# Latent attention's projections as split products: query, key and value weights in the common weight ring, cached keys split before the last path block

## The chip, the cores and the metric

The kernel runs on one core of one Trainium2 chip. The metric is the device time of one launch in microseconds (us). TensorE (PE in the profile, its weight loads PEld) does the matrix products, VectorE (DVE) and ScalarE (ACT) the elementwise work and most copies out of PSUM, GpSimd (POOL) a share of the elementwise work between SBUF tiles, and SyncE (SP) issues most transfers. SBUF is the working memory on the chip, PSUM the accumulators that TensorE writes.

## The reference

Two layers of a hybrid block are applied to 512 latent and 128 context tokens, in 32-bit floats. Three branches are fed by one input projection: a long convolution, a differential attention and multi-head latent attention (MLA). Each is multiplied by a gate, projected, and merged. The change is in MLA:

```
c_q  = rms_norm(mla_dq, q_norm)                    # (tokens, 384)
qm   = (c_q @ w_uq).reshape(n, 8, 64 + 32)         # q_nope | q_rope
c_kv = rms_norm(mla_dkv, kv_norm)                  # (tokens, 256)
ckv_all = concat([cached_ckv, c_kv])               # latent tokens: 128 cached rows + 512
kv   = (ckv_all @ w_ukv).reshape(n, 8, 64 + 64)    # k_nope | v
s    = (q_nope . k_nope + rope(q_rope) . rope(k_rope)) * scale
y    = softmax(s) @ v
```

## The kernel before

Everything is stored with features on the 128 partitions and the 640 tokens along the free side. A matrix product of 32-bit floats is done in one of two ways.

Split products. `project` (L806) takes a weight block of 128 output features by 1024 (or 512) inputs. The weights come into a ring `W` of three buffers (`weight`, L665, by SP). ScalarE writes the high part `Wh` in the type float32r (`high_part`, L1213), and GpSimd (for a few blocks VectorE) the low part `Wl` = W - Wh (`low_part`, L1963). The activations are split in the same way beforehand (`Hh`, `Hl` for the layer's input, `BRh`, `BRl` for a gated branch). For each input block and each half of 320 tokens there are three products: Wh.xh (L817), Wh.xl (L818), and, after a wait for the low part, Wl.xh (L822). `Wh` and `Wl` have two buffers, so the high part of block n+1 waits for block n-1 to be done (`tile_done`). The ring buffer is loaded again when its low part is written.

Direct products. Attention, transposes and, before the change, MLA's own projections pass 32-bit tiles to TensorE as they are. `mqr` (rotary part, 2 blocks of 128 features) and `mqn` (other part, 4 blocks) multiply `wuq` by `cq` (L1140), `mk` (4 blocks) and `mv` (3 steps of two token blocks) multiply `wukv` by `ckv` (L1148, L1129). Their weights are loaded whole, once in a layer, at step (dqkv, 3).

Order. `layer_steps` writes the order of a layer out by hand as a list of steps, and every engine runs through this one list, doing its part of each step. Around the change it is:

```
... dqkv 3, mms 0, dqkv 4, kr, mms 1, path 4, mrt, path 5, path 6, mb 0, mb 1,
    path 7, cc, sc, mv 0..2, mqr 0, mqn 0, mqh 0, mk 0, ml_score 0, ...
```

`path 4..7` are blocks of the gate for the second branch. ScalarE takes tanh of each from PSUM (L1350), VectorE multiplies and writes `BRh` (L1758, L1760, L1764), GpSimd writes `BRl`. `mb` multiplies by the norm's reciprocal root (VectorE, L1882), `cc` transposes the cached rows, `sc` the new context rows for the output. In the attention that follows, the merge blocks `mgate` and `mbranch` of the second branch stand between the scores of eight heads, and `mqr`, `mqn`, `mqh`, `mk` of the next heads too.

When the high part of block n+1 is made is set by `upto_table` (L407). With a and b the places of blocks n and n+1 in the list, the high part stands ahead of ScalarE's own work of step a if b - a <= 2 ("near"), and else behind it, at step a+1. GpSimd's low part has the same place. In GpSimd's program of a path step, `BRl` comes behind a low part of that place and ahead of a low part of the next one.

Of the kernel before, what the change touches and what calls it, by code (L numbers as in the profile page):

```python
# [15 lines left out]
DEPTH, D, LAT, CTX, PAST = 2, 1024, 512, 128, 128  # L16
# [121 lines left out]
def layer_steps(l):  # L138
# [32 lines left out]
    s += p[:1] + [("mrt", 0)] + p[1:3] + [("mb", 0), ("mb", 1)] + p[3:] + [("cc", 0), ("sc", 0)]  # L171
# [58 lines left out]
SPLIT_AT = {step: n for n, step in enumerate(SPLIT)}  # L230

def spectrum_user(n, j):
# [4 lines left out]
    if z:  # L239
# [41 lines left out]
    "cc": lambda i: [("cc_ready", 2)],  # L281
    "mms": lambda i: [("m_ms", i + 1)],
    "mb": lambda i: [("c_ready", i + 1)],
# [31 lines left out]
           pad_ready=1, lam_sum=1, lam_exp=1, c_ready=2, sc_ready=1, mv_ready=3, mqr_raw=2, mqn_ready=8, mq_ready=8, mk_ready=8, ml_max=40, ml_exp=40, ml_p=40,  # L315
# [107 lines left out]
def build(nc, A, O):  # L423
# [10 lines left out]
    with ctx:  # L434
# [58 lines left out]
        WORK = 20640  # L493
# [62 lines left out]
        wukv = area(work, 10624, 2, 1024)  # L556
        mq_lat = [area(work, off, LAT) for off in (12672, 12672 + NTOK, 11136)]
        mq_ctx = [area(work, off, CTX) for off in (12672 + LAT, 12672 + NTOK + LAT, 20480)]
        rq, rq_ctx = area(work, 12160, LAT), area(work, 18048, CTX)
# [3 lines left out]
        wuq = area(work, 18176, 3, 768)  # L563
        sqm = area(work, 0, 3, NTOK)
        stc = area(work, 1920, KVL + MR)
        msm = area(work, 12672, HALF)
# [97 lines left out]
        N_CONSTS, N_SMALL, N_FILTER, N_DA, N_ML = 2, 2, 2, 3, 4  # L664

        @block.sync
        def _(sp):
            def weight(g):
# [5 lines left out]
                src = A[{"in": "w_in", "br": "w_branch", "out": "w_out"}[kind]][l, n]  # L674
# [56 lines left out]
            for l in range(DEPTH):  # L731
                for kind, i in STEPS[l]:
# [68 lines left out]
        def _(pe):  # L801
# [126 lines left out]
            for l in range(DEPTH):  # L928
                for kind, i in STEPS[l]:
# [184 lines left out]
                    elif kind == "sc":  # L1114
                        pe.wait_ge(*freed(l, kind, i))
                        ps = slot(l, kind, i)
                        pe.wait_ge(*after("c_ready", l, 2))
                        for c in range(2):
                            transpose(ps[:, 128 * c:128 * c + 128], ckv[:, c, LKEY:NKEY])
                        transpose(ps[:, 512:512 + MR], krs[:, LAT:NTOK], MR).then_inc(full_of(l, kind, i), 1)  # L1120
                    elif kind == "mv":
                        if i == 0:
                            pe.wait_ge(*after("cc_ready", l, 2))
                        pe.wait_ge(*freed(l, kind, i))
                        ps = slot(l, kind, i)
                        for b in range(2):
                            t = 2 * i + b
                            for k in range(2):
                                last = pe.matmul(  # L1129
                                    ps[:, 512 * b:512 * b + 512], ckv[:, k, 128 * t:128 * t + 128],  # L1130
                                    wukv[:, k, MH * MN:MH * (MN + MV)],
                                    start=k == 0, stop=k == 1)
                        last.then_inc(full_of(l, kind, i), 1)
                    elif kind in ("mqr", "mqn"):
                        pe.wait_ge(*freed(l, kind, i))
                        ps = slot(l, kind, i)
                        c0 = 128 * i + (MH * MN if kind == "mqr" else 0)
                        for t in (slice(0, LAT), slice(LAT, NTOK)):
                            for k in range(3):
                                last = pe.matmul(ps[:, t], wuq[:, k, c0:c0 + 128], cq[:, k, t], start=k == 0, stop=k == 2)  # L1140
                        last.then_inc(full_of(l, kind, i), 1)
                    elif kind == "mk":
                        pe.wait_ge(*freed(l, kind, i))
                        ps = slot(l, kind, i)
                        n_ = NKEY // 2
                        for a in range(2):
                            for k in range(2):
                                last = pe.matmul(  # L1148
                                    ps[:, 512 * a:512 * a + n_],
                                    wukv[:, k, 2 * MN * i:2 * MN * (i + 1)],  # L1150
                                    ckv[:, k, n_ * a:n_ * a + n_], start=k == 0, stop=k == 1)
# [33 lines left out]
        def _(act):  # L1185
# [31 lines left out]
            def high_part(l, n):  # L1217
# [8 lines left out]
                k = CT if SPLIT[n][0] == "mbranch" else KD  # L1226
                copy(Wh[:, n % 2, 0:k, :], W[:, g % NW, 0:k, :]).then_inc(sems["w_hi"], 1)

            for l in range(DEPTH):
                split = 2 if l else 0  # L1230
                for place, (kind, i) in enumerate(STEPS[l]):
# [172 lines left out]
                    elif kind == "cc":  # L1404
                        act.wait_ge(*filled(l, kind, i))
                        ps = slot(l, kind, i)
                        copy(ckv[:, :, 0:PAST], ps[:, 0:256].rearrange("p (a b) -> p a b", a=2)).then_inc(sems["cc_ready"], 1)
                        for b in range(2):
                            last = copy(mkT[64:96, b, 0:PAST], ps[0:MR, 512:640])
                        last.then_inc(sems["cc_ready"], 1)  # L1410
                    elif kind == "mrt":
# [13 lines left out]
                    elif kind == "mqr":  # L1425
# [4 lines left out]
                        copy(rq, ps[:, 0:LAT], MLA_SCALE)  # L1430
                        copy(rq_ctx, ps[:, LAT:NTOK], MLA_SCALE).then_inc(sems["mqr_raw"], 1)
# [660 lines left out]
```

## Time and profile before

| | us |
|---|---|
| median of 3 runs | 1925.38 (1922.63 to 1925.43) |
| the profiled execution | 1925.0 |
| its span in the profile | 1923.2 |
| PE / PEld busy | 1802.9 / 1572.3 |
| DVE / ACT / POOL busy | 1125.5 / 670.4 / 451.7 |

A busy time is the sum over the engine's instructions, overlaps taken once. In the timeline a row gives start, length, engine, line, operation and "out<-in", and in brackets how long the engine had been idle and what released it. Neighbouring equal instructions are merged, and then the length is of the group. The chain of waits gives start, length and line of what ended last. PEclk is the granted TensorE clock as a share of full speed. A 32-bit matmul shows as two records.

### The profile page before, as it was taken

What the parts mean: (1) busy time and instruction counts of PE and PEld (TensorE: products, weight loads), DVE (VectorE), ACT (ScalarE), POOL (GpSimd) and SP (SyncE); (2) the same over time, 40 slices, a digit from 0 to 9 for tenths busy, and PEclk for the clock granted to TensorE, in tenths of its full rate; (3) what the DMA queues carried; (4) which work ended last, traced back from release to release, by engine and by line L of the source; (5) the groups of instructions that cost most, each with busy time, mean ns of one, the idle gap of its engine ahead of it and who ended that gap; (6) DMA issues with size and microseconds to landing.
All of it is one profiled execution on the core that took longest, in us unless ns stands there. A gap on an engine that the chain in (4) does not pass through costs nothing.

```text
span 1923.2 us, 27833 instructions
## 1 busy us (share of the span) xinstructions
PE 1802.9 (94%) x11336; PEld 1572.3 (82%) x11336; DVE 1125.5 (59%) x1606; ACT 670.4 (35%) x1159; POOL 451.7 (23%) x208
## 2 busy tenths in 40 slices
PE   4999999999999999999989999999999999999997
PEld 3788799877786777899876969997879677779996
DVE  4689894445343444377877989925434343434755
ACT  3434312434234444321263342234433344442222
POOL 0100033222231111367300001322122211115561
PEclk8999999999999999999999999999999999999999
DMA  8111122211210111353621112221122011014431
GB/s 347 44 55 34 33 89 71 60 40 51 105 50 26 34 34 39 114 198 115 245 88 33 56 33 78 77 61 46 38 72 99 22 37 33 30 48 142 164 111 66
DMA packets 48622, 150.01 MB, mean 78 GB/s; under 512 B 9386, under 2 KB 11050, under 8 KB 47728
## 3 DMA queue, kind: packets, MB, share of 16 engines
q1 hardware_dynamic: 44896, 134.09, 20.3%
q10 hardware_dynamic: 3600, 14.16, 2.2%
q8 instruction: 90, 1.47, 0.3%
q14 instruction: 36, 0.29, 0.0%
HBM read 141.63 MB, written 6.59 MB: 77 GB/s over the span
## 4 chain that ended last, share of the span: by engine, by line
PE 66%; DVE 23%; issue 4%; ACT 4%; DMA 2%; POOL 1%; SPq 0%; ACTq 0%; DVEq 0%; POOLq 0%
PE PS L817 15%; PE PS L818 14%; PE PS L822 14%; PE PS L889 4%; PE PS L878 3%; PE PS L1140 2%; PE PS L923 2%; PE PS L920 2%; PE PS L1073 2%; PE PS L902 2%; DVE MG L1779 1%; DVE Wl L1546 1%; DVE st L1525 1%; DMA pmod_w<-in_w_mod 1%; PE PS L1129 1%
## 5 line engine op out<-in xcount | busy, mean ns | idle before, releaser
L1958 POOL TENSOR_TENSOR Wl<-W,Wh 128x1024 fp32r<-128x1024 f32 (+1 forms) x156 | 350.3, 2247 | 1291.9 <-ACT Wh L1193 1234.7
L817 PE MATMUL PS<-Hh,Wh 128*128 128x320 f32 x2048 | 613.5, 314 | 20.8 <-ACT Wh L1193 12.3
L818 PE MATMUL PS<-Hl,Wh 128*128 128x320 f32 x2048 | 604.9, 310 | 0.0
L817 PEld LDWEIGHTS PS<-Hh,Wh 128*128 128x128 f32 x2048 | 386.7, 189 | 45.9 <-issue 29.0
L818 PEld LDWEIGHTS PS<-Hl,Wh 128*128 128x128 f32 x2048 | 386.8, 189 | 0.6 <-issue 0.5
L822 PE MATMUL PS<-Hh,Wl 128*128 128x320 f32 x2048 | 321.4, 309 | 0.9 <-POOL Wl L1958 0.9
L822 PEld LDWEIGHTS PS<-Hh,Wl 128*128 128x128 f32 x2048 | 305.5, 188 | 1.5 <-POOL Wl L1958 1.5
L1525 DVE TENSOR_REDUCE st<-PS 128x1 f32<-128x640 f32 (+1 forms) x160 | 114.8, 718 | 315.1 <-PE PS L902 172.7
L1193 ACT ACTIVATE work<-PS 128x640 f32<-128x640 f32 (+9 forms) x298 | 172.6, 592 | 250.6 <-PE PS L822 64.2
L1193 ACT ACTIVATE Wh<-W 128x1024 fp32r<-128x1024 f32 (+1 forms) x188 | 176.4, 943 | 62.0 <-PE PS L822 26.8
L1350 ACT ACTIVATE th<-PS 128x640 f32<-128x640 f32 x64 | 45.1, 705 | 366.0 <-PE PS L822 366.0
L1193 ACT ACTIVATE raw<-PS 128x320 f32<-128x320 f32 (+4 forms) x98 | 38.1, 443 | 261.0 <-PE PS L822 188.6
L817 PE MATMUL PS<-BRh,Wh 128*128 128x320 f32 x384 | 116.4, 317 | 0.0
L818 PE MATMUL PS<-BRl,Wh 128*128 128x320 f32 x384 | 113.4, 309 | 0.0
L878 PE MATMUL PS<-fixed,work 128*128 128x128 f32 x580 | 88.5, 285 | 18.4 <-ACT work L1495 5.0
L878 PEld LDWEIGHTS PS<-fixed,work 128*128 128x128 f32 x580 | 72.7, 153 | 39.3 <-issue 12.8
L902 PE MATMUL PS<-work 96*128 96x320 f32 x256 | 81.0, 441 | 7.8 <-DVE MG L1779 4.5
L1604 DVE SCALAR_TENSOR_TENSOR raw<-work 128x1024 f32<-128x1024 f32 x46 | 82.4, 1792 | 7.6 <-DMA work<-in_w_mod_rows 6.1
L817 PEld LDWEIGHTS PS<-BRh,Wh 128*128 128x128 f32 x384 | 72.1, 188 | 7.0 <-ACT Wh L1193 6.1
L1375 ACT ACTIVATE work<-PS,st 128x640 f32<-128x640 f32 (+1 forms) x80 | 56.7, 710 | 55.7 <-DVE st L1525 55.7
L818 PEld LDWEIGHTS PS<-BRl,Wh 128*128 128x128 f32 x384 | 72.2, 188 | 0.0
L889 PE MATMUL PS<-work,MG 128*128 128x512 f32 x160 | 70.8, 594 | 1.0 <-ACT raw L1193 0.6
(234 smaller groups left out, 2502.8 us busy)
## 6 DMA issues: line engine op xcount, KB each, us to landing
W<-in_w_in SPq DMA_DIRECT2D x132, 512.0 KB, 3.5
W<-in_w_branch SPq DMA_DIRECT2D x48, 256.0 KB, 2.6
work<-in_w_mod_rows ACTq DMA_DIRECT2D x23, 512.0 KB, 3.7
pmod_w<-in_w_mod SPq DMA_DIRECT2D x8, 1024.0 KB, 14.4
W<-in_w_out SPq DMA_DIRECT2D x16, 512.0 KB, 4.5
work<-in_x_sample SPq DMA_DIRECT2D x2, 2048.0 KB
late_modulation_w<-in_w_mod_rows SPq DMA_DIRECT2D x5, 512.0 KB, 6.6
x_mid<-work SPq DMA_DIRECT2D x1, 2560.0 KB, 8.5
```

The source lines that it names most:

```text
L817: pe.matmul(out, Wh[:, b, kk, :], xh[:, kk, t], start=kk == 0, stop=False)
L818: pe.matmul(out, Wh[:, b, kk, :], xl[:, kk, t], start=False, stop=False)
L822: last = pe.matmul(out, Wl[:, b, kk, :], xh[:, kk, t], start=False, stop=kk == k - 1)
L878: return pe.transpose(out, in_, ident[0:p, 0:p])
L889: last = pe.matmul(ps[:, 512 * q:512 * q + HY], table, srcs[q ^ c][:, r, :], start=n_ == 0, stop=n_ == len(terms) - 1)
L902: last = pe.matmul(ps[:, 512 * a:512 * a + HALF], q_lat[:, 128 * t:128 * t + 128], k[:, HALF * a:HALF * a + HALF], start=True, stop=True)
L1193: return act.activation(out, in_, ACT.Copy, scale=scale)
L1350: act.activation(halves(th[:, n % 2]), two(ps), ACT.Tanh, scale=0.5)\
L1375: act.activation(two_or_one(e, n), two(ps) if n > CTX else ps[:, 0:n], ACT.Exp, bias=st[:, i % (LAG + 1), j:j + 1], accum_out=st[:, i % (L ...
L1525: return dve.tensor_reduce(out, two(ps) if n > CTX else ps[:, 0:n], mybir.AxisListType.XY if n > CTX else AX, ALU.max, negate=True)
L1604: ins = STT(mod_early if n < EARLY[l] else mod_late, modw[mod_buffer(l, n)], scale, cb[:, j], ALU.mult, ALU.mult, accum_out=modcs[:, at_ % ...
L1958: return pool.tensor_tensor(out, in_, high.bitcast(f32), ALU.subtract)
```

## The change

- `mqr`, `mqn`, `mk` and `mv` become split products. Their weights come through the ring: a new tile for each `mqr` and `mqn` (3 input blocks), for each `mk` (2), and one for all three `mv` steps (8 blocks' room). The loads of `wuq` and `wukv` go. A layer has 11 more tiles in the stream.
- `q_hi`, `q_lo`, `kv_hi`, `kv_lo` are new. ScalarE writes the high parts at `mb` (behind VectorE's norm) and at `cc`. VectorE writes the low parts at the new steps `clo` and at `cc`.
- `mb 1` (keys and values) now stands ahead of `mb 0` (queries), and both ahead of path 6. `cc` moves ahead of path 7. The order is path 4, mrt, path 5, mb 1, mb 0, path 6, clo 1, cc, path 7, clo 0, sc, mv 0..2.
- `mv 0` waits for its high and its low weights before its first product.
- `sc` reads a copy (`new_kv`). The copies behind `mqr` and `mqn` take both halves in one instruction.

```diff
-    s += p[:1] + [("mrt", 0)] + p[1:3] + [("mb", 0), ("mb", 1)] + p[3:] + [("cc", 0), ("sc", 0)]
+    s += p[:1] + [("mrt", 0)] + p[1:2] + [("mb", 1), ("mb", 0)] + p[2:3] + [("clo", 1), ("cc", 0)] + p[3:] + [("clo", 0), ("sc", 0)]
...
+    if kind in ("mqn", "mqr"):
+        return [("uq", i + 4 * (kind == "mqr"))]
+    if kind == "mk" or (kind == "mv" and i == 0):
+        return [("u" + kind[1], i)]
...
+def depth(kind):
+
+    return {"mbranch": CT, "mqn": 3, "mqr": 3, "mk": 2}.get(kind, KD)
...
         def tile_done(l, n):
 
             l, n = (l, n) if n >= 0 else (l - 1, n + NSPLIT)
+            if SPLIT[n] == ("mv", 0):
+                return filled(l, "mv", 2)
...
-                        for dst, src in ((wuq, A["mla_w_uq"][l].rearrange("(k p) n -> p k n", p=128)),
-                                         (wukv, A["mla_w_ukv"][l].rearrange("(k p) n -> p k n", p=128)),
-                                         (cc, A["cache_mla_ckv"][0, l]), (ckr, A["cache_mla_krope"][0, l])):
+                        for dst, src in ((cc, A["cache_mla_ckv"][0, l]), (ckr, A["cache_mla_krope"][0, l])):
...
                     elif kind == "mv":
+                        n = SPLIT_AT["mv", 0]
                         if i == 0:
-                            pe.wait_ge(*after("cc_ready", l, 2))
+                            pe.wait_ge(*after("c_lo", l, 2))
+                            pe.wait_ge(*after("w_hi", l, n + 1))
+                            pe.wait_ge(*after("w_lo", l, n + 1))
                         pe.wait_ge(*freed(l, kind, i))
                         ps = slot(l, kind, i)
+                        wide_h, wide_l = [w[:, n % 2].rearrange("p (k a) n -> p k (a n)", k=2) for w in (Wh, Wl)]
                         for b in range(2):
-                            t = 2 * i + b
+                            t, out = slice(256 * i + 128 * b, 256 * i + 128 * b + 128), ps[:, 512 * b:512 * b + 512]
                             for k in range(2):
-                                last = pe.matmul(
-                                    ps[:, 512 * b:512 * b + 512], ckv[:, k, 128 * t:128 * t + 128],
-                                    wukv[:, k, MH * MN:MH * (MN + MV)],
-                                    start=k == 0, stop=k == 1)
+                                pe.matmul(out, kv_hi[k][:, t], wide_h[:, k], start=k == 0, stop=False)
+                                pe.matmul(out, kv_hi[k][:, t], wide_l[:, k], start=False, stop=False)
+                                last = pe.matmul(out, kv_lo[:, k, t], wide_h[:, k], start=False, stop=k == 1)
                         last.then_inc(full_of(l, kind, i), 1)
                     elif kind in ("mqr", "mqn"):
...
+                        if (kind, i) == ("mqr", 0):
+                            pe.wait_ge(*after("c_lo", l, 3))
+                        project(l, kind, i, q_hi, q_lo, 3)
                     elif kind == "mk":
...
+                        pe.wait_ge(*after("w_hi", l, n + 1))
+                        for k in range(2):
+                            for out, t in outs:
+                                pe.matmul(out, Wh[:, n % 2, k, :], kv_hi[k][:, t], start=k == 0, stop=False)
+                                pe.matmul(out, Wh[:, n % 2, k, :], kv_lo[:, k, t], start=False, stop=False)
+                        pe.wait_ge(*after("w_lo", l, n + 1))
+                        for k in range(2):
+                            for out, t in outs:
+                                last = pe.matmul(out, Wl[:, n % 2, k, :], kv_hi[k][:, t], start=False, stop=k == 1)
...
+                    elif kind == "mb":
+                        act.wait_ge(*after("c_ready", l, 2 - i))
+                        if i:
+                            copy(new_kv, ckv[:, :, LKEY:NKEY])
+                            for k in range(2):
+                                copy(kv_hi[k][:, PAST:NKEY], ckv[:, k, PAST:NKEY]).then_inc(sems["c_hi"], 1)
+                        else:
+                            for k in range(3):
+                                copy(q_hi[:, k], cq[:, k]).then_inc(sems["c_hi"], 1)
...
+                    elif kind == "clo":
+                        dve.wait_ge(*after("c_hi", l, 2 if i else 5))
+                        for k in range(2 if i else 3):
+                            if i:
+                                last = TT(kv_lo[:, k, PAST:NKEY], ckv[:, k, PAST:NKEY], kv_hi[k][:, PAST:NKEY].bitcast(f32), ALU.subtract)
+                            else:
+                                last = TT(q_lo[:, k], cq[:, k], q_hi[:, k].bitcast(f32), ALU.subtract)
+                        last.then_inc(sems["c_lo"], 1)
+                        dve.wait_ge(*own("c_lo"))
```

## Rows read from the trace of the kernel before

**Rows 1.** The page: busy time by engine, and the chain by engine.

```profile
PE 1802.9 (94%) x11336; PEld 1572.3 (82%) x11336; DVE 1125.5 (59%) x1606; ACT 670.4 (35%) x1159; POOL 451.7 (23%) x208
PE 66%; DVE 23%; issue 4%; ACT 4%; DMA 2%; POOL 1%; SPq 0%; ACTq 0%; DVEq 0%; POOLq 0%
```

**Rows 2.** Chain of waits, layer 0, mv to mk (start, length, what).

```profile
574.33 10.57 PE PS L1129 x24
584.90 6.49 PE PS L1140 x24
591.39 2.60 PE PS L1148 x8
```

**Rows 3.** Chain row of 320-column split products; timeline of TensorE at 384 columns.

```profile
652.24 2.35 PE PS L822 x16
...
950.12 0.34 PE L853 MATMUL PS<-MGh,Oh 128*128 128x384 f32 x1
950.29 0.34 PE L854 MATMUL PS<-MGl,Oh 128*128 128x384 f32 x1
```

**Rows 4.** Timeline, layer 0, end of path 6 to mv 0.

```profile
562.14 0.70 ACT L1350 ACTIVATE th<-PS 128x640 f32<-128x640 f32 x1 [6.33 <-PE PS L822]
...
563.84 0.42 PE L817 MATMUL PS<-Hh,Wh 128*128 128x320 f32 x1 [0.99 <-ACT Wh L1193]
...
564.69 0.49 DVE L1764 CAST BRh<-th 128x640 fp32r<-128x640 f32 x1
565.22 4.17 DVE L1882 SCALAR_TENSOR_TENSOR work<-work,small,PS 128x640 f32<-128x640 f32 x5
565.26 1.58 POOL L1958 TENSOR_TENSOR BRl<-th,BRh 128x640 fp32r<-128x640 f32 x1 [5.46 <-DVE BRh L1764]
566.79 2.42 POOL L1958 TENSOR_TENSOR Wl<-W,Wh 128x1024 fp32r<-128x1024 f32 x1
...
569.26 2.61 PE L822 MATMUL PS<-Hh,Wl 128*128 128x320 f32 x16 [0.47 <-POOL Wl L1958]
...
571.91 0.70 ACT L1350 ACTIVATE th<-PS 128x640 f32<-128x640 f32 x1 [8.12 <-PE PS L822]
...
574.33 10.57 PE L1129 MATMUL PS<-work 128*128 128x512 f32 x24 [1.74 <-ACT work L1193]
```

**Rows 5.** Timeline, VectorE and GpSimd side by side, third branch and MLA.

```profile
808.45 1.23 DVE L1604 SCALAR_TENSOR_TENSOR raw<-work 128x1024 f32<-128x1024 f32 x1
808.49 2.62 POOL L1958 TENSOR_TENSOR BRl<-th,BRh 128x640 fp32r<-128x640 f32 x1 [3.03 <-DVE BRh L1764]
...
811.07 3.40 POOL L1958 TENSOR_TENSOR Wl<-W,Wh 128x1024 fp32r<-128x1024 f32 x1
...
611.08 2.38 POOL L1958 TENSOR_TENSOR Wl<-W,Wh 128x1024 fp32r<-128x1024 f32 x1 [2.90 <-ACT Wh L1193]
...
612.45 1.69 DVE L1779 TENSOR_TENSOR MG<-MG,th 128x640 f32<-128x640 f32 x1
```

**Rows 6.** Transposes in timeline and chain; stretches (from:to, length, PE busy, PEclk, DMA).

```profile
981.56 4.30 PE L878 MATMUL PS<-fixed,work 128*128 128x128 f32 x20 [5.03 <-ACT work L1495]
...
607.20 0.55 PE PS L878 x5
...
510.00:520.00 10.00, 8.74 (x57) 0.83 0.19 60
...
784.00:790.00 6.00, 3.52 (x29) 1.00 0.27 98
1724.00:1730.00 6.00, 3.52 (x18) 0.72 0.26 87
```

**Rows 7.** Timeline rows of ScalarE around mk in the attention, chain row of mk.

```profile
631.01 0.62 ACT L1193 ACTIVATE Wh<-W 128x512 fp32r<-128x512 f32 x1
...
632.54 2.58 PE PS L1148 x8
...
633.81 0.69 ACT L1193 ACTIVATE work<-PS 128x640 f32<-128x640 f32 x1
```

More of the change, by code:

```diff
@@ L280 @@
     "kr": lambda i: [("kr_raw", 1)],
[L281 removed]
+    "cc": lambda i: [("c_lo", 2)],
+    "clo": lambda i: [],
     "mms": lambda i: [("m_ms", i + 1)],
[L283 removed]
+    "mb": lambda i: [("c_ready", 2 - i)],
     "sc": lambda i: [("sc_ready", 1)],
@@ L555, in build @@
         mkT = area(work, 9088, 2, NKEY)
[L556 to L559, printed above, removed]
+        mq = [area(work, off, NTOK) for off in (12672, 12672 + NTOK, 10624)]
+        mq_lat, mq_ctx = [q[:, 0:LAT] for q in mq], [q[:, LAT:NTOK] for q in mq]
+        rq_all = area(work, 11264, NTOK)
+        rq, rq_ctx = rq_all[:, 0:LAT], rq_all[:, LAT:NTOK]
+        kv_hi = [sb(f"kv_hi{k}", [128, NKEY], f32r, over=work_at + 4 * off) for k, off in enumerate((11904, 18048))]
+        kv_lo = sb("kv_lo", [128, 2, NKEY], f32r, over=work_at + 4 * 4480)
+        q_hi = sb("q_hi", [128, 3, NTOK], f32r, over=work_at + 4 * 18816)
+        q_lo = sb("q_lo", [128, 3, NTOK], f32r, over=work_at + 4 * 2560)
         Em = [area(work, 13952, NTOK), area(work, 13952 + NTOK, NTOK), raw[:, 0, 0:NTOK]]
@@ L1133, in _ @@
                         last.then_inc(full_of(l, kind, i), 1)
                     elif kind in ("mqr", "mqn"):
[L1135 to L1140, printed above, removed]
@@ L1144, in _ @@
                         ps = slot(l, kind, i)
[L1145 to L1151, printed above, removed]
+                        n, n_ = SPLIT_AT["mk", i], NKEY // 2
+                        outs = [(ps[:, 512 * a:512 * a + n_], slice(n_ * a, n_ * a + n_)) for a in range(2)]
+                        pe.wait_ge(*after("w_hi", l, n + 1))
[7 more added lines that the diff above has]
+                                last = pe.matmul(out, Wl[:, n % 2, k, :], kv_hi[k][:, t], start=False, stop=k == 1)
                         last.then_inc(full_of(l, kind, i), 1)
@@ L1429, in _ @@
                             act.wait_ge(*after("mq_ready", l, 4 * i))
-                        copy(rq, ps[:, 0:LAT], MLA_SCALE)
-                        copy(rq_ctx, ps[:, LAT:NTOK], MLA_SCALE).then_inc(sems["mqr_raw"], 1)
+                        copy(halves(rq_all), two(ps), MLA_SCALE).then_inc(sems["mqr_raw"], 1)
                     elif kind == "mqn":
@@ L1884, in _ @@
                         dve.wait_ge(*own("c_ready"))
+                    elif kind == "clo":
[7 more added lines that the diff above has]
+                        dve.wait_ge(*own("c_lo"))
+                    elif kind == "cc":
+                        dve.wait_ge(*filled(l, kind, i))
+                        dve.wait_ge(*after("cc_ready", l, 2))
+                        for k in range(2):
+                            last = TT(kv_lo[:, k, 0:PAST], slot(l, kind, i)[:, 128 * k:128 * k + 128], kv_hi[k][:, 0:PAST].bitcast(f32),
+                                      ALU.subtract)
+                        last.then_inc(sems["c_lo"], 1)
+                        dve.wait_ge(*own("c_lo"))
                     elif kind == "mqr":
@@ L2058, in laid_out @@
         "c_rows": np.stack([x["c"][0], x["c_ctx"]]),
[L2060 to L2062 removed]
+        "mla_uq": tiles(np.concatenate([x["mla_w_uq"].reshape(DEPTH, QL, MH, MN + MR)[..., part].reshape(DEPTH, QL, -1)
+                                        for part in (slice(0, MN), slice(MN, MN + MR))], -1)),
+        "mla_uk": tiles(ukv[..., 0, :].reshape(DEPTH, KVL, -1)),
+        "mla_uv": ukv[..., 1, :].reshape(DEPTH, 2, 128, MH * MV).transpose(0, 2, 1, 3).reshape(DEPTH, 1, 128, KD, 128),
         "w_in": tiles(np.concatenate([w_in[:, :, :3 * HY], heads_first(w_in[:, :, 3 * HY:3 * HY + 512]),
```

30 lines of the change are left out of this document (14 added, 16 removed).

## Prediction, made before the changed kernel was run

> **What bounds the kernel now.** I read the page first. TensorE is busy 94% of the span, and two thirds of the chain that ended last are TensorE's [rows 1]. So products that get shorter are worth their time, unless TensorE then waits for somebody. Next I read the chain through MLA's start: mv, mqr with mqn, and mk follow each other without a gap and wait for no weights [rows 2]. Last I read the timeline ahead of it, the end of path 6 to mv 0, because the change puts new split tiles and new waits there [rows 4]. The reader is to see two patterns in those rows. Behind a path block that is followed by small steps, the next block's high part is made only after the tanh, and its low part only after GpSimd has written BRl, which waits for three VectorE instructions.
>
> **Part 1, the products.** An mv step takes 10.57 / 3 = 3.52 us, mqr and mqn together 6.49 us, so 3.24 each, and mk 2.60 [rows 2]. A split product of 320 columns starts every 2.35 / 16 = 0.147 us, one of 384 every 0.17 [rows 3]. For 512 columns there is no row: scaled by columns from the one at 384 it is 0.227, from the one at 320 it is 0.235. I take 0.227, the nearer. Then mv has 12 products, 2.72 us, and saves 0.8. mqr and mqn have 18, 2.64 us, and save 0.6. mk has 12, 2.08 us, and saves 0.5. In a layer that is 3 x 0.8 + 6 x 0.6 + 4 x 0.5 = 8.0 us, 16 us in all, if nothing waits. Of it 2.4 + 1.2 + 0.5 = 4.1 lie ahead of the first scores and 3.9 between the heads.
>
> **Part 2, the path blocks.** The time between two tanhs is 571.91 - 562.14 = 9.77 us around path 7 [rows 4], where a block without waits is 48 x 0.147 = 7.05. The 2.7 us more are the wait for the high part (TensorE starts 1.70 after the tanh) and for the low part (its products start 7.12 after the tanh, though the others would be through 1.70 + 4.70 = 6.40 after it) [rows 4]. Before, mb stands ahead of path 7 alone, and path 6 is near path 5. After, path 6 has mb 1 and mb 0 ahead of it and path 7 has clo 1 and cc, so both lose the 2.7. One of them is new: +2.7. The few products of mb and cc hide in these waits, as mb's do now.
>
> **Part 3, mv's weights.** Now mv 0 starts 574.33 - 571.91 = 2.4 us behind the tanh of path 7 and waits only for the copies of cc [rows 4]. After the change it waits for a low part that GpSimd makes behind BRl of path 7. That is the pattern of path 7's own low part, 7.12 behind the tanh [rows 4]: +4.7. Nothing covers it. On TensorE the whole list is queued behind the wait, and only sc (0.5 us) stands ahead.
>
> **Part 4, the low parts of the activations.** clo 1 is two and clo 0 three VectorE instructions with both inputs in SBUF, started just when GpSimd starts BRl. The nearest row: with such an instruction of 1.23 us ahead of it, BRl takes 2.62 us instead of 1.58, and the low part behind it 3.40 instead of 2.42 [rows 4, 5]. Each waits for one VectorE instruction. The five instructions of mb, which read PSUM, leave BRl at 1.58 [rows 4]. Ours have 640 columns. The one at 612.45 takes 1.69 us, but GpSimd's ends at 613.46, so 0.7 are its own [rows 5], and mb's are 4.17 / 5 = 0.83 [rows 4]. I take 0.8 on BRl and 0.8 on the low part, 1.6 at path 7 and 1.6 at mv 0: +3.2, between 0 and 3.2. The wait is at the end of clo, so clo's own time lies beside path 7 and the first mv steps. The Trainium skill (SBUF — State Buffer, section Who interferes with whom) says that a VectorE instruction with two SBUF inputs and a GpSimd instruction that reads SBUF block each other whole, the earlier one winning. It speaks against this placing of clo, and the rows agree; without it the sum would be lower by 6.4 us in two layers.
>
> So mv 0 starts 2.7 + 4.7 + 3.2 = 10.6 us later, and the first scores 10.6 - 4.1 = 6.5 later.
>
> **Part 5, the clock.** TensorE then stands still for about 8 us ahead of mv 0. After 5.03 us of idling 20 transposes took 4.30 us, 0.215 each, where five take 0.55 at full clock [rows 6]: the granted clock was at its lower level, 1.2 GHz, for all of them, and 2.1 us were lost. I take 2.1 for each layer, between 0 and 3. Besides, there are new stalls of 1 to 2.3 us at paths 6 and 7. One of 2.1 us lowered the clock in layer 1 (0.72 over 6 us) and not in layer 0 (1.00), and in 510 to 520 a fall cost 0.17 x 10 = 1.7 us [rows 6]. I take one fall more in the whole kernel, +1.7, between none and four.
>
> **Part 6, between the heads.** Three mqn save 0.6 each, 1.8. mk saves only 0.2 each: mbranch now follows mk as its neighbour in the ring, its high part (0.62 us) is made behind the transpose copy that ends at 634.5, so at about 635.1, and TensorE would be there at 635.12 - 0.5 [rows 7]. That is 0.6 from 0.5 x 3. mqr is followed by VectorE's rotation, on which the softmax hangs, and the low part for mqn now runs beside it: 0.1 of 0.6. On the other hand, behind two of the mbranch blocks VectorE's sum waits 0.8 us for GpSimd's low part of 1024 columns [rows 5], and that tile will be mqn's of 384, done before: 2 x 0.8 = 1.6. Together 4.1 less, between 2.5 and 5.
>
> At nothing I cost ScalarE's copies for kv_hi and q_hi: mb starts 3.1 us behind the tanh of path 5 and takes 4.2, three copies as long as a tanh (0.7) follow, so they end 9.4 behind it, and the next tanh comes at 9.77 [rows 4]; were that cover gone, a few tenths in each layer. The merged copies behind mqr and mqn and ScalarE's 11 more high parts lie beside products too, except the one named at mk. The ring's loads have two tiles' time and are as large as the loads removed. The small tiles' Wl waits are covered by the first two thirds of their own products.
>
> **The sum.** A layer: 10.6 - 4.1 + 2.1 - 4.1 = +4.5. Two layers +9.0, and 1.7 for the clock: +10.7. On the profiled execution's 1925.0 (0.4 under the median) that is 1935.7, and I say 1936.
>
> **Rivals.**
> (a) The low parts are not where I think, and the products show in full: -16, so 1909. It would need GpSimd free right behind path 7. For it speaks only that TensorE is the bound [rows 1]; against it that the same order of GpSimd's work is in the rows [rows 4]. Chance 0.12. Faster.
> (b) clo doesn't get in GpSimd's way (-6.4) and the clock costs half: 1936 - 6.4 - 2 = 1927.6, within 0.2%. For it: the arbitration row is of longer instructions. Chance 0.12, part of it above 1929.
> (c) The long idle is worse: the lower clock lasts 3 us more in each layer and falls at every new stall: +3 + 5, 1944. It would also be this if the heads gave nothing back (+8). Chance 0.12.
> (d) The forecast, 1930 to 1941: 0.64.
> The slower side decides from the point where the low part of mv 0 comes later than sc and 4.1 + 4.1 us of savings can pay, so from 8.2 us of delay in a layer; parts 2 and 3 alone give 7.4, and the clock or clo tips it.
>
> **Numbers.** A measurement of this kernel can tell 0.2%, 3.9 us, from no change. Faster by more has (a), 0.12. Within it falls most of (b), 0.10. Slower has (d), (c) and the rest: 0.78. The range that leaves out (a) and the upper part of (c) is 1926 to 1944.
>
> **What would show it.** In the profile after: the first of mv's products starts about 9 us behind the tanh of path 7, released by GpSimd's Wl, with some 8 us of idling and a granted clock under 1 behind it. BRl and Wl there take 2.3 and 3.2 us. Path 6 and path 7 are 9.8 and 11.4 us from tanh to tanh. mv takes 2.7 us a step at full clock, mqn 2.64, mk 2.08. The head parts are 4 us a layer shorter. If mv 0 starts less than 6 us behind the tanh, my reading of GpSimd's order is wrong, and with it the sign.

## The result, and the profile after

| | before | after |
|---|---|---|
| median | 1924.89 us (6 runs) | 1931.71 us (6 runs) |
| lowest to highest | 1922.63 to 1925.43 | 1929.86 to 1935.64 |
| ratio, 95% interval | | 1.0039 [1.0028, 1.0049] |
| span of the profiled execution | 1923.2 us | 1928.1 us |

The changed kernel is slower by 6.8 us, and by more than the 3.9 us that a measurement can tell from no change. (The ratio is not made of the two medians, whose quotient is 1.0035: by the means of the runs the difference is 7.7 us.) The forecast was +10.7, 1936, with a range of 1926 to 1944.

The page of the changed kernel, busy time and chain by engine, to be held against [rows 1], and two groups of its fifth part (busy time, mean ns, idle time before and what ended it):

```profile
PE 1790.6 (93%) x11464; PEld 1593.4 (83%) x11464; DVE 1155.3 (60%) x1620; ACT 685.1 (36%) x1175; POOL 480.8 (25%) x230
PE 63%; DVE 23%; issue 6%; ACT 4%; DMA 2%; POOL 1%; SPq 0%; ACTq 0%; DVEq 0%; POOLq 0%
...
L831 PE MATMUL PS<-Hh,Wh 128*128 128x320 f32 x2048 | 612.9, 314 | 22.9 <-ACT Wh L1210 14.3
...
L836 PE MATMUL PS<-Hh,Wl 128*128 128x320 f32 x2048 | 321.6, 309 | 4.2 <-POOL Wl L2001 4.2
```

TensorE has 12 us less work (1802.9 to 1790.6), although its mean granted clock was lower (0.978, before 0.983), and yet the kernel is longer. Its share of the chain fell from 66% to 63%. It waits for split parts. The timeline of the changed kernel, layer 0, from the tanh of path 6 to mv, shows where; it answers to [rows 4]:

```profile
563.39 0.70 ACT L1367 ACTIVATE th<-PS 128x640 f32<-128x640 f32 x1 [0.51 <-PE PS L836]
...
565.10 0.41 PE L831 MATMUL PS<-Hh,Wh 128*128 128x320 f32 x1 [1.41 <-ACT Wh L1210]
...
566.48 2.94 DVE L1915 TENSOR_TENSOR kv_lo<-work,kv_hi 128x640 fp32r<-128x640 f32 x2
566.53 2.22 POOL L2001 TENSOR_TENSOR BRl<-th,BRh 128x640 fp32r<-128x640 f32 x1 [5.84 <-DVE BRh L1790]
568.70 2.94 POOL L2001 TENSOR_TENSOR Wl<-W,Wh 128x1024 fp32r<-128x1024 f32 x1
...
571.70 2.62 PE L836 MATMUL PS<-Hh,Wl 128*128 128x320 f32 x16 [1.64 <-POOL Wl L2001]
574.35 0.70 ACT L1367 ACTIVATE th<-PS 128x640 f32<-128x640 f32 x1 [8.52 <-PE PS L836]
...
577.42 5.78 DVE L1917 TENSOR_TENSOR q_lo<-work,q_hi 128x640 fp32r<-128x640 f32 x3
577.47 2.17 POOL L2001 TENSOR_TENSOR BRl<-th,BRh 128x640 fp32r<-128x640 f32 x1 [5.83 <-DVE BRh L1790]
579.60 2.92 POOL L2001 TENSOR_TENSOR Wl<-W,Wh 128x1024 fp32r<-128x1024 f32 x1
...
582.78 0.76 PE L1147 MATMUL PS<-Wh,kv_hi 128*128 128x512 f32 x1 [8.07 <-POOL Wl L2001]
...
587.61 0.60 PE L1149 MATMUL PS<-Wh,kv_lo 128*128 128x512 f32 x1
...
588.03 0.42 PE L1147 MATMUL PS<-Wh,kv_hi 128*128 128x512 f32 x1
...
589.46 0.40 PE L1147 MATMUL PS<-Wh,kv_hi 128*128 128x512 f32 x1
589.70 0.39 PE L1148 MATMUL PS<-Wl,kv_hi 128*128 128x512 f32 x1
```

Read it from the bottom. The first of mv's products starts 8.43 us behind the tanh of path 7, and TensorE had been idle for 8.07. What it waited for is the last link of a chain on GpSimd: BRl, then Wl, both beside VectorE's three instructions for q_lo. The same is one block earlier in small (idle 1.41 for the high part, 1.64 for the low part). Until 588.03 mv's products start 0.43 apart, then 0.234: the clock was at its lower level, 1.2 GHz, for the first dozen. The granted clock of the two stretches around mv says it too (from:to, length, PE busy, PEclk, DMA share, GB/s):

```profile
576.00:592.00 16.00, 9.22 (x29) 0.68 0.05 11
...
1516.00:1534.00 18.00, 9.93 (x35) 0.72 0.03 10
```

The whole difference can be laid out by four marks of each layer: the tanh of path 5, mv 0, the first scores, and the last head's value products (probabilities times values), which stand last; their first product is the mark.

| stretch | before | after | difference |
|---|---|---|---|
| start to the tanh of path 4, layer 0 | 548.1 | 546.6 | -1.5 |
| tanh of path 5 to mv 0 | 19.23 | 29.17 | +9.9 |
| mv 0 to the first scores | 20.74 | 19.50 | -1.2 |
| first scores to the last head's value products | 193.4 | 189.1 | -4.3 |
| the last three rows in layer 1 | 233.5 | 237.8 | +4.3 |
| all the rest of the program | | | -2.3 |

A layer costs 4.4 us more, 8.7 in two. In all the other stretches the profiled execution was 3.8 us shorter than that of before, which leaves the 4.9 us between the spans. Of these 3.8 us 1.4 are one fall of the clock, right behind the last mark of layer 1. After a wait of 2.11 us there the granted clock was 0.72 over 6 us before [rows 6], and it is 1.00 from 1730 to 1736 us in the changed kernel. What is left is scatter between executions, as the repeats below show.

### The profile page after: what moved, and what is told of

It reads as the page before. It is cut to its first block, busy times and chain, and to the rows that moved or that the text cites. A ratio compares the mean times of both kernels' runs of the same rounds, so it can differ in the third digit from the quotient of the medians.

```text
span 1928.1 us, 28231 instructions
## 1 busy us (share of the span) xinstructions
PE 1790.6 (93%) x11464; PEld 1593.4 (83%) x11464; DVE 1155.3 (60%) x1620; ACT 685.1 (36%) x1175; POOL 480.8 (25%) x230
## 4 chain that ended last, share of the span: by engine, by line
PE 63%; DVE 23%; issue 6%; ACT 4%; DMA 2%; POOL 1%; SPq 0%; ACTq 0%; DVEq 0%; POOLq 0%
PE PS L831 15%; PE PS L832 14%; PE PS L836 14%; PE PS L903 4%; PE PS L892 3%; PE PS L937 2%; PE PS L934 2%; PE PS L1087 2%; DVE st L1551 2%; PE PS L916 2%; DVE Wl L1572 1%; DMA pmod_w<-in_w_mod 1%; DVE MG L1805 1%; ACT Wh L1210 1%; DVE work L1545 1%
## 5 line engine op out<-in xcount | busy, mean ns | idle before, releaser
L2001 POOL TENSOR_TENSOR Wl<-W,Wh 128x1024 fp32r<-128x1024 f32 (+3 forms) x178 | 376.3, 2115 | 1263.3 <-ACT Wh L1210 1206.1
L1210 ACT ACTIVATE work<-PS 128x640 f32<-128x640 f32 (+8 forms) x276 | 170.7, 625 | 253.0 <-PE PS L836 82.0
L1210 ACT ACTIVATE Wh<-W 128x1024 fp32r<-128x1024 f32 (+3 forms) x210 | 188.0, 899 | 63.5 <-PE PS L836 26.8
## 6 DMA issues: line engine op xcount, KB each, us to landing
pmod_w<-in_w_mod SPq DMA_DIRECT2D x8, 1024.0 KB, 13.8
```

What stands on the lines that cost most here:

```text
L1210: return act.activation(out, in_, ACT.Copy, scale=scale)
L2001: return pool.tensor_tensor(out, in_, high.bitcast(f32), ALU.subtract)
```

## The experiments

All runs had the kernel before beside them on the same chip (1924.25 us in the first four, 1924.32 in the next four, 1923.14 in the one beside the two repeats). "First scores" is the time from the tanh of path 5 to them: 39.97 us before, 48.7 after, in both layers.

**near7: the split parts of mv ahead of the tanh of path 7**

```diff
-            near = b - a <= 2 or (SPLIT[n][0] == "conv" and b - a <= 3) or SPLIT[n] == ("qk", 0)
+            near = b - a <= 2 or (SPLIT[n][0] == "conv" and b - a <= 3) or SPLIT[n] == ("qk", 0) or SPLIT[n] in (("path", 7),)
```

> The changed kernel with one line of the plan altered: the block behind path 7 (mv's weights) counts as near, so its high part stands ahead of ScalarE's tanh of path 7 and its low part ahead of GpSimd's BRl. Theory (the wait of mv 0 for the low part made behind BRl, and the clock that falls in it, take the gain): mv 0 starts under 1 us behind the tanh of path 7 instead of 8.4, the granted clock stays at its upper level there, so 8 + 2.4 = 10.4 us less in each layer: 1932 - 21 = 1911 us. Rival (the extra work of ScalarE, GpSimd and VectorE in and around the heads takes it): mv 0 moves but the time comes back later, 1925 to 1932 us.

Measured: 1917.87 us, ratio to before 0.9959 [0.9947, 0.9972]. The timeline of this kernel, the same place:

```profile
573.21 2.40 POOL L2001 TENSOR_TENSOR Wl<-W,Wh 128x1024 fp32r<-128x1024 f32 x1
...
575.95 0.70 ACT L1367 ACTIVATE th<-PS 128x640 f32<-128x640 f32 x1 [7.42 <-PE PS L836]
...
576.24 0.50 PE L1147 MATMUL PS<-Wh,kv_hi 128*128 128x512 f32 x1
```

mv 0 now starts 0.29 us behind the tanh, with no idle time before it, and the first scores come after 38.14 us, 10.5 less than in the changed kernel. The stall, its price and the sign of the change are shown by one line. The line moves the high part too, but that was not what mv 0 waited for: in the changed kernel ScalarE had it done at 576.00, 3.6 us before GpSimd began the low part. The time fell by 13.8 us of the 21 that two layers give. The other 7 went elsewhere: the stretch behind the first scores is 2.7 us longer in each layer, because the clock fell behind a wait of 2.10 us in both (665 and 1600), for twice as long in layer 0, and behind another at 1718, where it had not in the changed kernel. This is the wait, here in the timeline of the changed kernel; TensorE waits there for VectorE behind the rotation of mqr 1:

```profile
674.06 0.33 PE L892 MATMUL PS<-fixed,raw 128*128 128x128 f32 x1 [2.10 <-DVE raw L1579]
```

The runs keep_busy and high_first_busy and the two repeats take that up.

**near567: the same for the followers of paths 5, 6 and 7**

```diff
-            near = b - a <= 2 or (SPLIT[n][0] == "conv" and b - a <= 3) or SPLIT[n] == ("qk", 0)
+            near = b - a <= 2 or (SPLIT[n][0] == "conv" and b - a <= 3) or SPLIT[n] == ("qk", 0) or SPLIT[n] in (("path", 5), ("path", 6), ("path", 7))
```

> As e1_near7, and the blocks behind path 5 and path 6 count as near too. Theory: besides e1's gain the tanhs of paths 5, 6 and 7 follow each other at 7.05 us plus the few products between (0.8 of mb, 0.3 of cc) instead of 9.8 and 11.0, so 2 + 3.6 = 5.6 us less in each layer: 1911 - 11 = 1900 us. Rival (TensorE then waits for something else that is late at the same place, the norm's products or ScalarE's copies): under 4 us less than e1.

Measured: 1911.57 us, 0.9931 [0.9919, 0.9944]; the first scores after 36.57, only 1.6 less than in near7. The timeline of this kernel around the tanh of path 6:

```profile
561.53 1.99 ACT L1210 ACTIVATE q_hi<-work 128x640 fp32r<-128x640 f32 x3 [0.82 <-DVE work L1908]
563.43 1.04 ACT L1210 ACTIVATE Wh<-W 128x1024 fp32r<-128x1024 f32 x1
...
564.52 0.41 PE L831 MATMUL PS<-Hh,Wh 128*128 128x320 f32 x1 [1.99 <-ACT Wh L1210]
```

The high part of path 7 now stands ahead of the tanh of path 6, but behind ScalarE's copies for kv_hi and q_hi, and these wait for VectorE's mb. TensorE waits 1.99 us for it. That is less than the four waits of 4.5 us in all (0.99, 0.47, 1.41 and 1.64) that near7 still has between the tanh of path 5 and mv 0, but behind this one the clock fell (0.50 from 564.8 to 568.2 us, 0.72 from 564 to 570), and that took back up to 1.7. So a part of the stall moved from one queue to the other. My number had left out what stands in ScalarE's queue at that place.

**clo_apart: VectorE's low parts where GpSimd is idle**

```diff
                         dve.wait_ge(*own("c_ready"))
+                        if i == 0:
+                            dve.wait_ge(*after("c_hi", l, 2))
+                            for k in range(2):
...
+                            last.then_inc(sems["c_lo"], 1)
+                            dve.wait_ge(*own("c_lo"))
                     elif kind == "clo":
-                        dve.wait_ge(*after("c_hi", l, 2 if i else 5))
+                        if i:
+                            continue
+                        dve.wait_ge(*after("c_hi", l, 5))
+                        dve.wait_ge(*after("w_lo", l, SPLIT_AT["mv", 0] + 1))
```

> The changed kernel, with VectorE's two kv_lo instructions moved from behind path 6 to behind mb 0, and its three q_lo instructions held back until GpSimd has made mv's low part. Nothing else moves. Theory (VectorE instructions with both inputs in SBUF hold GpSimd up): BRl and Wl at paths 6 and 7 take 1.58 and 2.42 us again instead of 2.2 and 2.9, so 4 x 1.1 = 4.5 us less in all: 1927 us. Rival (they only overlap it, the wait is from something else): within 1 us of 1932.

Measured: 1930.3 us, 1.0031 [1.0019, 1.0043]. The timeline of this kernel, GpSimd and VectorE:

```profile
562.89 1.56 DVE L1914 TENSOR_TENSOR kv_lo<-work,kv_hi 128x640 fp32r<-128x640 f32 x2
...
568.50 1.57 POOL L2010 TENSOR_TENSOR BRl<-th,BRh 128x640 fp32r<-128x640 f32 x1 [5.84 <-DVE BRh L1790]
...
570.03 2.39 POOL L2010 TENSOR_TENSOR Wl<-W,Wh 128x1024 fp32r<-128x1024 f32 x1
...
578.24 1.53 POOL L2010 TENSOR_TENSOR BRl<-th,BRh 128x640 fp32r<-128x640 f32 x1 [5.82 <-DVE BRh L1790]
579.73 2.34 POOL L2010 TENSOR_TENSOR Wl<-W,Wh 128x1024 fp32r<-128x1024 f32 x1
...
582.33 0.77 PE L1147 MATMUL PS<-Wh,kv_hi 128*128 128x512 f32 x1 [6.85 <-POOL Wl L2010]
```

Apart, BRl and Wl take 1.57 and 2.39 us at path 7 and 1.53 and 2.34 at mv 0; together with clo they took 2.22 and 2.94, 2.17 and 2.92. The two pairs differ by 1.2 us each, and mv 0 starts 26.7 instead of 29.2 us behind the tanh of path 5, 2.4 less, as these add up to. That the two engines hold each other up, and its price on the path, is shown. In the time only 1.4 us of the 5 arrived; the clock fell behind waits at 790, 1614 and 1732 where it stayed up in the changed kernel's profile, and behind the first scores the two layers are 3.9 us longer.

**keep_busy: products without use ahead of mv 0**

```diff
                         if i == 0:
+                            pe.wait_ge(*freed(l, kind, i))
+                            for kk in range(24):
+                                for a in range(2):
+                                    pe.matmul(slot(l, kind, i)[:, 512 * a:512 * a + HALF], Wh[:, (n - 1) % 2, kk % KD, :],
+                                              Hh[:, kk % KD, HALF * a:HALF * a + HALF], start=True, stop=True)
                             pe.wait_ge(*after("c_lo", l, 2))
```

> The changed kernel, with 48 products of 320 columns (7.05 us) that nobody reads ahead of mv 0's wait for its weights; they lie in the 8 us in which TensorE stood still. Theory (the idle stretch lowers the granted clock and that costs 2.4 us in each layer): mv 0 starts when it did, runs at 0.234 us a product from the first one, 1932 - 4.8 = 1927 us. Rival (the lower clock comes from the waits of paths 6 and 7 and falls all the same, or the loss is caught up in the heads): 1931 to 1933 us.

Measured: 1930.2 us, 1.0028 [1.0019, 1.0037]. The timeline of this kernel:

```profile
574.45 7.30 PE L1141 MATMUL PS<-Hh,Wh 128*128 128x320 f32 x48
...
582.68 0.47 PE L1152 MATMUL PS<-Wh,kv_hi 128*128 128x512 f32 x1 [0.94 <-POOL Wl L2006]
583.00 0.39 PE L1153 MATMUL PS<-Wl,kv_hi 128*128 128x512 f32 x1
583.23 0.39 PE L1154 MATMUL PS<-Wh,kv_lo 128*128 128x512 f32 x1
```

mv 0 starts where it did, but its products are 0.234 apart from the start, and the first scores come 2.3 us earlier in each layer. So the idling of 8 us costs 2.3 us more than itself. Of the 4.7 in two layers 1.5 arrived in the time. The rest is found again: behind the same 2.10 us wait as in near7 the clock fell in both layers (673 and 1615 us), and from the first scores to the last value product each layer takes 1.6 us longer than in the changed kernel.

**before_near and before_order: the kernel before, with one part each**

```diff
-            near = b - a <= 2 or (SPLIT[n][0] == "conv" and b - a <= 3) or SPLIT[n] == ("qk", 0)
+            near = b - a <= 2 or (SPLIT[n][0] == "conv" and b - a <= 3) or SPLIT[n] == ("qk", 0) or SPLIT[n] in (("path", 6), ("path", 7))
```

```diff
-    s += p[:1] + [("mrt", 0)] + p[1:3] + [("mb", 0), ("mb", 1)] + p[3:] + [("cc", 0), ("sc", 0)]
+    s += p[:1] + [("mrt", 0)] + p[1:2] + [("mb", 1), ("mb", 0)] + p[2:3] + [("clo", 1), ("cc", 0)] + p[3:] + [("clo", 0), ("sc", 0)]
```

The first is before_near. In before_order, the second, the steps clo are empty.

> The kernel before, with the split parts of path 7 made ahead of the tanh of path 6, and those of path 7's follower ahead of the tanh of path 7. My theory says that a block whose parts are made behind the tanh costs 2.7 us more than the 7.05 us of its products, and that this is independent of the change: path 6 to path 7 goes from 9.77 to some 7.1 us between the tanhs, less what ScalarE's and VectorE's own queues give back, so 1.9 to 2.7 us less in a layer, 1919.5 to 1921. The rival, that TensorE in this place is held by mb's VectorE work and by the copies of cc and not by the order of the parts, expects the first scores at the same place and 1925.

> The kernel before with its whole fp32 products and its own weights, and only the new order of the steps: mb 1 and mb 0 ahead of path 6, cc ahead of path 7, sc behind it. If the order alone costs the 2.7 us of a second path block with its parts behind the tanh, the time between the tanhs of path 5 and path 6 goes from 7.0 to 9.8 us and mv 0 starts less than 2.7 us later (cc is no longer behind path 7, which gives back up to 1.7): +1 to +2.7 us in a layer, 1926.5 to 1930. The rival, that the delay at path 6 comes from the split of the activations and not from the order, expects 9.8 not to be seen and 1922 to 1925.

Measured: before_near 1916.14 us, 0.9961 [0.9948, 0.9973]; before_order 1923.7 us, 0.9996 [0.9987, 1.0005]. The timelines, first of before_near, then of before_order:

```profile
563.46 0.70 ACT L1350 ACTIVATE th<-PS 128x640 f32<-128x640 f32 x1 [5.39 <-PE PS L822]
...
571.45 0.70 ACT L1350 ACTIVATE th<-PS 128x640 f32<-128x640 f32 x1 [6.34 <-PE PS L822]
```

```profile
555.83 0.70 ACT L1351 ACTIVATE th<-PS 128x640 f32<-128x640 f32 x1 [3.25 <-PE PS L823]
...
557.53 0.41 PE L818 MATMUL PS<-Hh,Wh 128*128 128x320 f32 x1 [0.99 <-ACT Wh L1194]
...
565.59 0.70 ACT L1351 ACTIVATE th<-PS 128x640 f32<-128x640 f32 x1 [8.11 <-PE PS L823]
```

In before_near the block takes 7.99 us from tanh to tanh instead of the 9.77 of [rows 4], and the first scores come after 37.25 us, 2.7 less. The pattern of Part 2 was in the kernel before as well, and one line takes it away. The time is below the 1919.5 to 1921 that I expected, 8.2 us less for the 5.4 of two layers; its profile lacks the fall at 1726 that the kernel before had (1.4 us). In before_order path 6 takes 9.76, as the forecast had it for the new order alone, without any split. But the first scores come only 0.57 us later: with cc ahead of path 7, mv 0 starts 0.29 behind its tanh and not 2.4. I had given back 1.7 at most and it gave 2.1, so the order is nearly free (+0.6 in a layer), and the expectation of 1926.5 to 1930 was too high. What is left of the changed kernel's delay, 48.67 - 40.54 = 8.1 us, is the split weights and activations: TensorE waits for their parts (9.4 us more up to mv 0, and 1.2 less behind it).

**high_first: every split part ahead of ScalarE's other work**

```diff
+        table[l, STEPS[l].index(("path", 5))] = SPLIT_AT["path", 6] + 1
+        table[l, STEPS[l].index(("mb", 1))] = SPLIT_AT["path", 7] + 1
+        table[l, STEPS[l].index(("clo", 1))] = SPLIT_AT["mv", 0] + 1
```

with clo as in clo_apart.

> The changed kernel with the split parts of path 6 made ahead of the tanh of path 5, those of path 7 directly behind that tanh and ahead of ScalarE's kv_hi and q_hi copies, those of mv behind the tanh of path 6, and clo 1 on VectorE directly behind mb 0, clo 0 behind mv's low part. My theory says that the whole loss in this stretch is waiting for split parts: path 5 to 6 and 6 to 7 then take 7.1 us each from tanh to tanh where near567 had 10.1 and 9.0, mv 0 starts within 1.5 us of the last path block, the clock does not fall at path 7, and the time is 1911.6 - 2 x 5 - 1.7 = 1900. The rival, that ScalarE is full in this stretch (tanhs, copies, split parts), has the tanhs late whatever the order, and expects 3 us less gain in a layer: 1906.

Measured: 1905.17 us, 0.9903 [0.989, 0.9917], the fastest kernel of all these. A grouped view of TensorE from 554 to 573 us in this kernel (busy, mean ns, idle before):

```profile
L834 PE MATMUL PS<-Hh,Wh 128*128 128x320 f32 x32 | 9.6, 315 | 0.0
...
L839 PE MATMUL PS<-Hh,Wl 128*128 128x320 f32 x36 | 5.8, 309 | 0.0
L1150 PE MATMUL PS<-Wh,kv_hi 128*128 128x512 f32 x3 | 1.3, 419 | 0.8 <-POOL Wl L2013 0.8
```

TensorE waits for 0.8 us in the whole stretch. The first scores come after 33.57 us, 3.0 less than in near567, not 5, so the number is the rival's. Its reason is not: the tanh of path 6 is late (9.2 us behind that of path 5, since ScalarE copies q_hi first), but nobody waits for it. My 5 set both blocks at 7.1 us, their own products alone. From the tanh of path 5 to that of path 7 high_first takes 15.4 us and not 14.2, since the small products of mb and cc lie between, and mv 0 starts 1.1 behind the last tanh and not 0.3: these are the missing 2. On TensorE's own side the 3.0 are the waits (1.99 us in near567, 0.8 here) and the fall of the clock behind the longer one, up to 1.7.

**high_first_busy: where the missing gains go**

```diff
                     elif kind == "ml_ptrans":
+                        if i == 14:
+                            pe.wait_ge(*freed(l, kind, i))
+                            for kk in range(14):
+                                pe.matmul(slot(l, kind, i)[:, 0:HALF], q_hi[:, kk % 3, 0:128], q_hi[:, kk % 3, 0:HALF], start=True, stop=True)
                         pe.wait_ge(*after("ml_p", l, i + 1))
```

> The kernel of the run high_first, with 14 products of 320 columns (2.06 us, their result is overwritten) where TensorE otherwise waits 2.10 us for VectorE's reciprocal behind the rotation of mqr 1. They cost nothing while the wait lasts. If part of what the local changes win is given back because the clock falls behind this wait, the granted clock stays up there and the time is 1.7 to 3.4 us below that of high_first. The rival, that a fall that is kept away here comes at the next short wait instead, expects the same time within 1 us.

Measured: 1905.03 us, 0.99 [0.9886, 0.9913], the same as high_first. Stretches of high_first, then of high_first_busy (PEclk is the fourth number):

```profile
656.00:676.00 20.00, 17.68 (x108) 0.91 0.13 40
776.00:792.00 16.00, 13.57 (x96) 1.00 0.34 123
...
1002.00:1018.00 16.00, 16.00 (x97) 1.00 0.20 67
```

```profile
656.00:676.00 20.00, 19.73 (x128) 1.00 0.15 46
776.00:792.00 16.00, 13.52 (x87) 0.89 0.20 67
...
1002.00:1018.00 16.00, 15.77 (x89) 0.89 0.19 67
```

The fall at 660 us is gone (0.91 to 1.00), and the one at 1588 too. In their place the clock fell behind the next wait of 2.11 us in both layers, at 779 and at 1708. (The one at 1002 came in the repeat of high_first as well and is no effect of this edit.) The rival was right in the time: what one short wait no longer loses, another one lost. That covering the one brought on the other is not shown; one profile of this kernel was taken.

**Two repeats: is the list of falls a kernel's own?**

> The changed kernel, unaltered, with a second profile. In its first one the granted clock fell at 482, 512, 576, 960, 980, 1420, 1454 and 1518 us and not behind the 2.10 us waits at 674 and 1616, where it fell in other kernels with the same wait. If falls behind such short waits are set by the kernel's own instructions, the second profile shows the same list within 2 us. If they hang on how the wait lies to something outside the kernel, at least one fall at a short wait is there in one profile and not in the other, while the long ones at mv 0 are in both.

> The kernel of the run high_first, unaltered, with a second profile. The same two readings: the first profile has falls at 660 and 1588, both behind the 2.10 us wait after mqr 1, and none at 780 and 1002. A list fixed by the kernel repeats these; one that is not shows at least one of them gone or another one come.

Measured: spans of 1931.0 and 1904.2 us, where the first profiles had 1928.1 and 1902.1. The same stretches, first of the changed kernel, then of its repeat:

```profile
656.00:676.00 20.00, 17.68 (x115) 1.00 0.14 47
...
956.00:966.00 10.00, 8.20 (x41) 0.83 0.14 51
1002.00:1018.00 16.00, 13.96 (x82) 1.00 0.11 33
```

```profile
656.00:676.00 20.00, 18.33 (x121) 1.00 0.15 47
...
956.00:966.00 10.00, 8.13 (x47) 1.00 0.15 54
1002.00:1018.00 16.00, 13.95 (x72) 0.89 0.09 28
```

Both readings are partly right. The long falls at mv are in both (0.68 from 576 to 592 us in both, as shown above for the first). The one at 956 to 966 us is in one profile and not in the other, the one at 1002 to 1018 the other way round. In the repeat of high_first a fall at 1000 came that the first had not, while its falls at 660 and 1588 were there again (662 and 1590). Behind the same 2.10 us wait the changed kernel's clock stayed up in both layers of both its profiles. So a short wait may or may not be followed by a fall, and part of it changes from one execution to the next. What decides it stays open.

What the falls cost can be added up all the same. In this table both layers are taken together, against the changed kernel's first profile (the stretch behind the first scores is up to the last value product, 191.4 us a layer in both of its profiles):

| run | first scores earlier | stretch behind them longer | left | time less |
|---|---|---|---|---|
| near7 | 21.2 | 5.4 | 15.7 | 13.8 |
| near567 | 24.3 | 3.1 | 21.2 | 20.1 |
| clo_apart | 5.0 | 3.9 | 1.1 | 1.4 |
| keep_busy | 4.7 | 3.2 | 1.6 | 1.5 |
| high_first | 30.3 | 3.1 | 27.2 | 26.5 |

So most of what did not arrive went in the attention of the same layer, behind its two waits of 2.1 us. In near567, keep_busy and high_first, with one fall in each layer there, a fall costs 1.55 us; the changed kernel has none there. Behind the wait of 2.10 us the clock fell in all ten layers of the five profiles in which it was up at mv (near7, near567, keep_busy, high_first twice), and in one of the six layers of the three in which it had fallen at mv (the changed kernel twice, clo_apart). Eight profiles don't show whether the one keeps away the other. In the kernel before the wait is 1.72 us, and neither there nor in before_near and before_order did the clock fall behind it.

Up to the first scores there is no such scatter: those of the repeat come after 48.73 and 48.67 us, those of the first profile after 48.67 and 48.76.

## Why the prediction was right

The sign, the place and the mechanism came out as forecast; the range held.

- **Part 1, the products.** mv's start 0.234 us apart at full clock, the bound from 320 columns, so a step is 2.80 us and not 2.72. mqr and mqn are as forecast, 0.147 for each product. Between mv 0 and the first scores near7, which has full clock there, is 3.6 us shorter than the kernel before (17.14 against 20.74), forecast 4.1. Here the forecast was 0.5 too good, and all of it is mv: from its first product to mqr's it takes 10.4 us before and 8.5 in near7, 1.9 less and not 2.4.
- **Part 2, the path blocks.** Path 6 takes 9.78 us from tanh to tanh, forecast 9.8; path 7 takes 10.96, forecast 11.4. before_order shows that the first is the order's alone. ScalarE's copies, costed at nothing, did end in time: q_hi at 562.88, 0.51 us ahead of the tanh of path 6.
- **Part 3, mv's weights.** mv 0 starts 8.43 us behind the tanh of path 7, forecast 8.7, released by GpSimd's Wl as forecast. near7 shows that this order of the work is the cause. Without clo it is 7.20 (clo_apart), so the term of +4.7 was 4.8.
- **Part 4, clo and GpSimd.** The term that was too large: 1.2 us a pair and not 1.6, as clo_apart isolates. I had let each GpSimd instruction wait for a whole VectorE instruction of 0.8; BRl lost 0.64 and Wl 0.58 at mv 0. With Parts 2 and 3 this gives 9.9 us of delay at mv 0 (29.17 - 19.23) for the 10.6 of the forecast. The rule quoted from the Trainium skill (SBUF — State Buffer, section Who interferes with whom) has the right sign, and the trace agrees with "whole" too. Taken one by one, the five instructions end in turn: q_lo 578.25, BRl 579.64, q_lo 580.32, Wl 582.52, q_lo 583.20. From one end to the next are 1.39, 0.68, 2.20 and 0.68 us, each 0.14 or 0.15 less than the instruction takes alone (1.53, 0.83, 2.34, 0.83). So each waited until the other was done, and only some 0.15 us of it ran beside the other. q_lo had 0.78 and 0.72 us left when BRl and Wl began; less 0.14 these are the 0.64 and 0.58.
- **Part 5, the clock.** 2.3 us a layer by keep_busy; in the changed kernel 12.3 of mv's products at 0.43 instead of 0.234 are 2.4. Forecast 2.1. The one more fall that I had put in (+1.7) isn't there: by the falls at short waits the changed kernel's profile is no worse than the one before.
- **Part 6, between the heads.** 4.3 and 4.5 us less, forecast 4.1. The pieces fit too. Cut layer 0 at the first value product of each head: of the eight pieces from the first scores on, two are 1.4 us shorter, one 0.8, three 0.25 and the last two not at all. The forecast had 0.6 + 0.8 for an mqn with the sum behind mbranch, 0.6 + 0.1 for an mqn with mqr, and 0.2 for an mk. The sum behind mbranch is no longer held up by the low part. The timeline of the changed kernel shows 0.83 where [rows 5] has 1.69:

```profile
617.77 1.02 POOL L2001 TENSOR_TENSOR Wl<-W,Wh 128x384 fp32r<-128x384 f32 x1 [2.36 <-ACT Wh L1210]
...
619.67 0.83 DVE L1805 TENSOR_TENSOR MG<-MG,th 128x640 f32<-128x640 f32 x1
```

A layer then is 9.9 - 3.6 + 2.4 - 4.3 = +4.4, forecast 4.5. That it is so near is luck in part: the errors in Parts 1, 4 and 5 are of 0.3 to 0.8 us and cancelled. The time came 3.9 us under the forecast. 1.7 is the fall that did not come. 1.4 is, if the profiles stand for the other executions, the fall at 1726 that the kernel before had and the changed one has in neither profile; I had not put it in. The last 0.8 is within what executions differ by: all that lies outside the two stretches from the tanh of path 5 to the last value product took 1450.4 us before, and 1447.9 and 1450.8 in the two profiles of the changed kernel.

Rival (a) named GpSimd free behind path 7 as its condition, with 1909. near7, which makes mv's parts early, came to 1917.9, and high_first to 1905.2. Against before_near, the kernel before with its own parts early, the split products are worth 1916.1 - 1905.2 = 11 us, with two falls of 1.55 us already taken off: that is about the gain that the changed kernel had in hand and waited away. The 16 us of the rival came together in no run.

## What to carry to other kernels

Before products are made shorter by splitting their operands, follow who makes the split parts, in which queue, and behind what: a part that is made behind the last nonlinearity of the block before cost some 8 us of TensorE's time in a layer here, as much as the 36 products of mv behind it (36 x 0.234 = 8.4). Move the making of the part ahead of the consumer's predecessor, and then look again at the queue that it went into, because near567 found the next stall there. Work out what TensorE gains from TensorE's own marks; the distance between two instructions of another engine can hold time that nobody waited for.

## What the runs showed of the hardware

- After 8.07 us without work TensorE's next dozen products ran at 1.2 GHz, 5.2 us long; useless products during the wait kept it at 2.4 GHz, worth 2.3 us. Waits of 2.1 us, the same in place and length, were followed by a fall in some kernels and executions and not in others, and a fall cost 1.4 to 1.6 us. Covering one didn't shorten the kernel. Of the local gains in two layers 66% showed in the time in near7 (13.8 of 21), 30% in clo_apart and keep_busy (1.4 and 1.5 of some 5), but more than all in before_near (8.2 of 5.4): falls in the two layers' attention, there or not, are a large part of the difference (5.4 of 7 us in near7, all of it in clo_apart and keep_busy, 1.4 of 2.8 in before_near).
- VectorE and GpSimd, both with SBUF operands, took turns instruction by instruction, with some 0.15 us of overlap. Two VectorE instructions of 640 columns took 1.56 us alone and 2.94 beside GpSimd, three took 2.30 alone (582.20 to 584.50 in clo_apart) and 5.78 beside it. GpSimd's pair grew from 3.96 to 5.16 and from 3.87 to 5.09. So beside two the losses are alike (1.4 and 1.2 us), and beside three VectorE, whose instructions are the shorter ones, lost most (3.5 and 1.2).
- A split product of 512 columns starts every 0.234 us at full clock, in line with 0.147 for 320.
